# A decoder layer with a sparse expert FFN: x handed over turned, small inputs packed, the first projection unit in four pieces

## The chip, the cores and the metric

One core of a Trainium2 chip. The metric is the device time of one execution in microseconds (us). Engines: PE (TensorE, matmul; PEld its weight loads), DVE (VectorE), ACT (ScalarE), POOL (GpSimd), SP (SyncE, which only issues transfers here); SPq and ACTq are the issues of transfers from SP's and ACT's instruction streams. Each of the two has a queue of its own, and all transfers run on the core's 16 DMA engines.

## The reference

```python
h = rms_norm(x, attn_norm_g)                     # x: 256 tokens x 1024, float32
z = h @ w_in                                     # 1024 x 3640, one combined projection
(c_q, c_kv, k_pe, q_b, k_b, v_b, q_idx, k_idx, w_idx, gate_a, gate_b) = split_cols(z, IN_SPLITS)
y_a = mla_branch(...)                            # latent attention, 8 heads, causal
y_b = dsa_branch(...)                            # indexer scores -> 64 keys a query -> attention
merged = sigmoid(gate_a) * (y_a @ w_branch_mla) + sigmoid(gate_b) * (y_b @ w_branch_dsa)
x = x + merged @ w_out
x = x + moe_ffn(rms_norm(x, ffn_norm_g), ...)    # top 4 of 32 experts, 1024 -> 2x1024 -> 1024, with biases
return rms_norm(x, final_norm_g)
```

All is float32. The experts' weights are 32 x 12.6 MB, some 400 MB in all; the rest of the weights is about 25 MB.

## The kernel before, in words

The kernel is written engine by engine, with semaphores by hand; each engine runs its own list in the order written, so an engine waits where its list says.

*Front.* Tokens are two tiles t of 128 (`xs`). The model dimension is split into 8 slices c of 128; x and `w_in` are cut so that partition p holds elements 8p+c. The kernel needs h turned (`hT`, model dimension on the partitions). The scale 1/rms of a token is left out of h and is applied when a product leaves its PSUM bank; only the gain is multiplied in. So `turn_x(t)` (L631) turns tile t of x by 8 PE transposes with the identity into two banks, and DVE's `hidden(t)` (L1442) multiplies the two banks by `g_in` into `hT`. The combined projection is done in units of up to 512 columns: unit 0 is q_idx (512), unit 1 k_b, v_b, k_idx and w_idx (200 columns), unit 2 q_b (512), unit 3 c_q, c_kv and k_pe (416). `z_unit(n)` (L647) does, for each tile, 8 products of 128x128 by 128 x width into a bank of `ZB`; float32 makes each of them two passes in the trace. Unit 0's weights are loaded in three pieces (`Z_FIRST`, L74), and tile 1 of x is turned between slices 5 and 6 of tile 0. ACT's `z_evac(n)` (L1193) copies the banks out, scaled by the token's 1/rms; the bank of tile t of unit n has to be free (`z_ok`) before unit n+1 uses it. The scale comes from ACT (`Square` of x with a sum, L1180; root, L1189) and DVE (`x_rstd`, L1448). Between tile 0 and tile 1 of this, DVE works out the rotary angles from the positions and a second block of constants (L1460 to L1479), and ACT's list has both tiles' scales ahead of its first eviction. Two short products spread the scales over a row (`spread_rstd`, L638). PE runs ten passes on zeros at the start and four more behind the first turn (`open_clock`, L622).

*Small inputs.* ACT's queue brings the identity and `g_in` at once, the positions (two loads of one column) and the second constants behind the square of tile 0. SP's queue brings, in this order (L451, L487 to L502): x tile 0, the three pieces of unit 0, x tile 1, the constants ones and slot, unit 1 (two loads, strided rows), the gate-up biases in four loads, `g_q`, `g_kv`, the router's bias, units 2 and 3, `g_tok`, `b_down` four times, the up-projection weights (two loads), then gate, branch and output weights as slots of a ring of six come free. The gate-up biases (32 experts x 2048) are turned by four PE transposes between units 1 and 2 (L727 to L730) and put in their place (`bias_gu`) by two DVE copies (L1495). The router's weights and, column by column, `g_ffn` are loaded in the middle of the expert weights (L514 to L516) and multiplied together by DVE at L1623.

*Rest of the front.* Index scores, a top-64 search on DVE, up-projections, both attentions with gate products filled in between, branch products (L855), the output projection (L879), the residual, the router's logits (L894), the routing, and the gather of the first expert's tokens.

*Experts.* Each expert item takes up to 64 tokens: 4 units of gate-up weights and 2 of down weights, 2 MB each, through twelve slots that lie over the front's tiles. SP issues a load when PE has read the slot's last contents (`used`); before that, at L503 to L529, single loads are issued as parts of the front are finished with, the last one behind the logits (`lg_ps`, L528). Then `load_round` (L531) goes on with half and quarter loads behind the first products of the first expert (L556 to L562).

## Time and profile before

| | |
|---|---|
| runs, us | 1112.34, 1111.98, 1112.65; median 1112.34 |
| span of the profiled execution, us | 1110.8 |
| around the span, against the median, us | 1.5 |
| PE busy | 1075.1 us, 97% |
| DVE / ACT / POOL busy | 279.6 / 166.4 / 21.6 us |
| transferred | 431.67 MB, mean 389 GB/s |

The page gives the span of the profiled execution alone, not its own time with what lies around it. In the views, an engine's line reads: start, length, engine, line of the kernel, operation, written tile <- read tiles, number of instructions, and in brackets the idle time of the engine before it with what ended it. PE's ends are modelled, so "busy" can hold short waits. "issue" is time in which an engine waited for nothing that the profile shows.

### The profile page before, as it was taken

The numbers are of one execution on the slowest core, as the hardware profiler recorded it, in microseconds if no ns is written. First come the engines' busy times: TensorE is split into PE (matmuls) and PEld (weight loads), VectorE is DVE, ScalarE is ACT, GpSimd is POOL, SyncE is SP. The second block draws the span as 40 slices with busy tenths as digits, with TensorE's granted clock in tenths as the row PEclk, the third lists the DMA queues.
The fourth block names the chain that finished last, engine by engine and source line by source line (L and its number), as shares of the span: only waits on it lengthen the run. The fifth ranks groups of instructions, "written<-read, shape, count | busy, mean of one in ns | idle before, by whom it ended". The sixth has DMA issues, their size and how long they took to land.

```text
span 1110.8 us, 13188 instructions
## 1 busy us (share of the span) xinstructions
PE 1075.1 (97%) x5066; PEld 463.1 (42%) x5066; DVE 279.6 (25%) x658; ACT 166.4 (15%) x352; POOL 21.6 (2%) x44
## 2 busy tenths in 40 slices
PE   9999999999999999999999999999999999999997
PEld 6578786533333333333333333333333333333333
DVE  2167432322222222222222222222221111222112
ACT  2144430210110001101100100000000000000002
POOL 0121100000000000000000000000000000000000
PEclk9999999999999999999999999999999999999999
DMA  9934645899999999999999999999999999999997
GB/s 314 357 105 159 258 167 223 323 409 432 431 432 431 430 432 432 429 434 432 429 432 432 430 431 432 430 431 432 432 429 434 432 430 432 432 430 431 432 426 295
DMA packets 48085, 431.67 MB, mean 389 GB/s; under 512 B 8256, under 2 KB 10688, under 8 KB 23232
## 3 DMA queue, kind: packets, MB, share of 16 engines
q1 hardware_dynamic: 47200, 430.91, 92.4%
q10 hardware_dynamic: 864, 0.47, 0.1%
q8 instruction: 14, 0.23, 0.1%
q14 instruction: 7, 0.06, 0.0%
HBM read 430.32 MB, written 1.05 MB: 388 GB/s over the span
## 4 chain that ended last, share of the span: by engine, by line
PE 67%; DMA 22%; SPq 9%; DVE 1%; issue 0%; POOL 0%; ACT 0%; another core or an unknown queue 0%; POOLq 0%; DVEq 0%
PE bank L1033 26%; DMA raw<-in_w_gate_up 22%; PE bank L1056 12%; PE bank L615 8%; SPq L482 7%; PE bank L619 5%; PE bank L668 4%; PE bank L1005 3%; PE bank L955 3%; PE bank L883 2%; SPq L485 2%; PE bank L1072 1%; PE bank L689 1%; PE bank L677 0%; DMA cst<-in_consts 0%
## 5 line engine op out<-in xcount | busy, mean ns | idle before, releaser
L1033 PE MATMUL bank<-raw,xT 128*64 128x512 f32 x2048 | 461.9, 596 | 26.1 <-DMA raw<-in_w_gate_up 25.5
L1033 PEld LDWEIGHTS bank<-raw,xT 128*64 128x64 f32 x2048 | 141.5, 137 | 318.5 <-issue 264.9
L1056 PE MATMUL bank<-raw,actT 128*64 128x512 f32 x992 | 225.2, 595 | 0.0
L1056 PEld LDWEIGHTS bank<-raw,actT 128*64 128x64 f32 x992 | 68.7, 137 | 127.6 <-issue 119.0
L1693 DVE TENSOR_SCALAR gated<-cst,posc,gates 128x128 f32<-128x128 f32 x64 | 19.3, 344 | 278.2 <-PE bank L1005 278.2
L1744 DVE TENSOR_TENSOR gub<-bank,bias_gu 128x512 f32<-128x512 f32 x64 | 43.9, 685 | 160.4 <-PE bank L619 160.4
L1751 DVE COPY ev_gu<-bank 128x512 f32<-128x512 f32 x32 | 22.1, 692 | 219.4 <-PE bank L1033 219.4
L1352 ACT COPY ev_gu<-bank 128x512 f32<-128x512 f32 x32 | 18.7, 585 | 373.9 <-PE bank L1033 373.9
L1005 PE MATMUL bank<-ev,gated 64*128 64x512 f32 x248 | 61.6, 615 | 0.0
L615 PE MATMUL bank<-hT,front_raw 128*128 128x256 f32 x256 | 58.7, 382 | 0.0
L955 PE MATMUL bank<-x_res,onehot 128*64 128x512 f32 x248 | 58.5, 592 | 0.0
L615 PEld LDWEIGHTS bank<-hT,front_raw 128*128 128x128 f32 x256 | 47.4, 190 | 8.1 <-issue 2.3
L668 PE MATMUL bank<-front_raw,hT 128*128 128x512 f32 (+2 forms) x128 | 45.7, 516 | 0.0
L619 PEld LDWEIGHTS bank<-cst,ev_gu 128*128 128x128 f32 x256 | 33.4, 210 | 25.2 <-issue 25.2
L1357 ACT ACTIVATE ev_gu<-gub 128x512 f32<-128x512 f32 x32 | 20.1, 630 | 151.9 <-DVE gub L1758 151.9
L619 PE MATMUL bank<-cst,ev_gu 128*128 128x128 f32 x256 | 39.3, 297 | 0.0
L1005 PEld LDWEIGHTS bank<-ev,gated 64*128 64x128 f32 x248 | 21.3, 186 | 39.3 <-issue 39.3
L955 PEld LDWEIGHTS bank<-x_res,onehot 128*64 128x64 f32 x248 | 17.9, 137 | 35.3 <-issue 35.3
L668 PEld LDWEIGHTS bank<-front_raw,hT 128*128 128x128 f32 x128 | 23.9, 195 | 19.7 <-issue 19.4
L1362 ACT COPY ev<-bank 128x512 f32<-128x512 f32 x31 | 18.2, 586 | 81.6 <-PE bank L1056 81.6
L1331 ACT COPY ev<-bank 128x512 f32<-128x512 f32 x31 | 18.1, 585 | 73.3 <-PE bank L955 73.3
L1345 ACT COPY gated<-bank 128x256 f32<-128x256 f32 x32 | 11.9, 372 | 113.0 <-PE bank L619 113.0
(248 smaller groups left out, 598.9 us busy)
## 6 DMA issues: line engine op xcount, KB each, us to landing
raw<-in_w_gate_up SPq DMA_DIRECT2D x123, 2048.0 KB, 44.0
raw<-in_w_down SPq DMA_DIRECT2D x60, 2048.0 KB, 43.8
front_raw<-in_w_in SPq DMA_DIRECT2D x5, 2048.0 KB, 15.8
raw<-in_w_gate_up SPq DMA_DIRECT2D x9, 1024.0 KB, 9.2
raw<-in_w_down SPq DMA_DIRECT2D x12, 512.0 KB, 17.9
front_raw<-in_w_out SPq DMA_DIRECT2D x2, 2048.0 KB, 9.7
front_raw<-in_w_branch_mla SPq DMA_DIRECT2D x1, 2048.0 KB, 8.8
front_raw<-in_w_branch_dsa SPq DMA_DIRECT2D x1, 2048.0 KB, 7.8
```

Of the source, the lines that this page charges most:

```text
L482: sp.dma_start(raw[:, slot, :], w_gu_v[e, u // 2, :, u % 2 * UNIT:(u % 2 + 1) * UNIT]).then_inc(raw_in[slot], 16)
L485: sp.dma_start(raw[:, slot, :], w_dn_v[e, u]).then_inc(raw_in[slot], 16)
L615: mm = pe.matmul(o, lhs(c), rhs(c), start=start and c == 0, stop=c == n - 1)
L619: return pe.transpose(o, src, ident)
L668: mm = pe.matmul(ZB[t][:, 0:w], hT[:, c, t * P:(t + 1) * P], unit3(n, w)[:, c, :], start=c == 0, stop=c == KC - 1)
L883: mm = pe.matmul(B[2 * t + n][:, :], mT[:, c, t * P:(t + 1) * P], unit3(U_WO + n)[:, c, :], start=c == 0, stop=c == KC - 1)
L955: mm = pe.matmul(PREP[half * SLOTS:(half + 1) * SLOTS, :], onehot[:, t, :], xs[:, t, half * BLK:(half + 1) * BLK], start=t == 0, stop=t == ...
L1005: mm = pe.matmul(ACC[2 * t + half][:, :], scat[rows, t * P:(t + 1) * P], ev[rows, :], start=False, stop=True, skip_group_check=True)
L1033: mm = pe.matmul(GU[pair][half * SLOTS:(half + 1) * SLOTS, :], xT[:, c, b, :], w[:, at:at + BLK], start=u == 0 and k == 0, stop=last and k ...
L1056: mm = pe.matmul(DN[half * SLOTS:(half + 1) * SLOTS, :], actT[:, c, u, :], w[:, at:at + BLK], start=u == 0 and c == 0, stop=u == DN_UNITS ...
L1744: dve.tensor_tensor(gub[:, pair, :].rearrange("p (j s) -> p j s", s=SLOTS), GU[pair][:, :].rearrange("p (j s) -> p j s", s=SLOTS), bias_gu ...
L1751: dve.tensor_copy(ev_gu[:, 1, :], GU[1][:, :]).then_inc(lin_ev, 1)
```

## The change

The host hands the kernel other arrays (`laid_out`): x a second time, turned to partition p, slice c, token; `w_in` unit by unit, so that a unit is one contiguous row a partition; both up-projection weights in one array; the positions as one 128x2 array; the gate-up biases in the order of `bias_gu`; and `g_q`, `g_kv`, `g_ffn`, the router's bias and its weights in one array `packed`. On the chip, `hT` is loaded from the turned x in four pieces from ACT's queue and multiplied by `g_in` in place, slice by slice, for both tiles at once. PE's transposes of x and of the biases, the second `open_clock`, and the DVE copies of the biases go. Unit 0 comes in four pieces, in the order of the slices, each used for both tiles. Tile 0 of x is issued behind the third piece.

```diff
-Z_FIRST = (slice(0, 2), slice(2, 4), slice(4, KC))
+Z_FIRST = (slice(0, 1), slice(1, 2), slice(2, 4), slice(4, KC))
+IN_UNITS = Z_UNITS + [[(GATES_AT + k * BLK, BLK)] for k in range(4)]
+PACK = {"g_q": 2, "g_kv": 1, "g_ffn": KC, "rb": EXPERTS, "rw": KC * EXPERTS}
+def laid_out(inputs):
+    w = a["w_in"][0].reshape(P, KC, D_IN)
+    units = [np.concatenate([w[:, :, c0:c0 + n] for c0, n in part], axis=2).reshape(P, -1) for part in IN_UNITS]
...
+        "x_turned": a["x"][0].reshape(TOKENS, P, KC).transpose(1, 2, 0).reshape(P, KC * TOKENS),
+        "positions": a["positions"][0].reshape(TT, P).T,
+        "w_in": np.concatenate(units, axis=1),
+        "w_up": np.concatenate([a["mla_w_uq"][0].reshape(P, UP_Q), a["mla_w_ukv"][0]], axis=1),
+        "b_gate_up": a["b_gate_up"][0].reshape(EXPERTS, 2, 2, P, 4).transpose(3, 0, 1, 4, 2).reshape(P, EXPERTS * 16),
...
         def _(sp):
-            sp.dma_start(xs[:, 0, :], x[0, 0:P, :]).then_inc(x_in[0], 16)
...
-            load_front(0)
+            for cs, landed in zip(Z_FIRST, (*z_part, raw_in[0])):
+                sp.dma_start(unit3(0)[:, cs, :], w_in_v(0)[:, cs, :]).then_inc(landed, 16)
+                if cs.stop == KC // 2:
+                    sp.dma_start(xs[:, 0, :], x[0, 0:P, :]).then_inc(x_in[0], 16)
             sp.dma_start(xs[:, 1, :], x[0, P:2 * P, :]).then_inc(x_in[1], 16)
-            sp.dma_start(cst[:, P:KEPT], consts[:, P:KEPT]).then_inc(rest_in, 16)
             load_front(1)
-            for q in range(4):
-                sp.dma_start(bgu[q * EXPERTS:(q + 1) * EXPERTS, :], b_gate_up[0, :, q * BLK:(q + 1) * BLK]).then_inc(small_in, 16)
-            sp.dma_start(g_q[:, :], ...)
-            sp.dma_start(g_kv[:, :], ...)
-            sp.dma_start(rb[:, :], ...)
+            sp.dma_start(pack[:, :], packed).then_inc(small_in, 16)
             load_front(2)
             load_front(3)
             sp.dma_start(g_tok[:, :, :], ffn_norm_g[0].rearrange("(h p c) -> p h c", h=2, c=4)).then_inc(bd_in, 16)
+            sp.dma_start(bias_gu[:, :, :].rearrange("p e j -> p (e j)"), b_gate_up).then_inc(bias_in, 16)
...
-            sp.dma_start(rw[:, :, :], router_w[0].rearrange("(c p) n -> p c n", p=P)).then_inc(router_in, 16)
-            for c in range(KC):
-                sp.dma_start(g_ffn[:, c:c + 1], ...).then_inc(router_in, 16)
...
+            def first_z():
+                for cs, landed in zip(Z_FIRST[:-1], z_part):
+                    pe.wait_ge(landed, 16)
+                    for c in range(cs.start, cs.stop):
+                        pe.wait_ge(hT_ok, c + 1)
+                        for t in range(TT):
+                            z_product(0, t, c)
+                landed_front(pe, 0)
+                for t in range(TT):
+                    for c in range(Z_FIRST[-1].start, KC):
+                        if t == 0:
+                            pe.wait_ge(hT_ok, c + 1)
+                        mm = z_product(0, t, c)
+                    mm.then_inc(z_ps, 1)
...
-                    if t == 0 and n == 0:
-                        turn_x(0)
-                        open_clock(2)
...
-                        if n == 0 and t == 0 and c == 6:
-                            turn_x(1)
...
-            pe.wait_ge(small_in, SMALL)
-            for c in range(4):
-                tr = turned(B[7][:, c * P:(c + 1) * P], bgu[:, c:BLK:4])
-            tr.then_inc(bgu_ps, 1)
...
         def _(act):
-            act.dma_start(cst[:, 0:P], consts[:, 0:P]).then_inc(cst_in, 16)
-            act.dma_start(g_in[:, :], attn_norm_g[0].rearrange("(p c) -> p c", c=KC)).then_inc(g_in_in, 16)
+            act.dma_start(hT[:, Z_FIRST[0], :], xt_v[:, Z_FIRST[0], :]).then_inc(xt_in[0], 16)
+            act.dma_start(g_in[:, :], attn_norm_g).then_inc(g_in_in, 16)
+            for cs, landed in zip(Z_FIRST[1:], xt_in[1:]):
+                act.dma_start(hT[:, cs, :], xt_v[:, cs, :]).then_inc(landed, 16)
+            act.dma_start(cst[:, :], consts[:, 0:KEPT]).then_inc(cst_in, 16)
...
                 if t == 0:
-                    for k in range(TT):
-                        act.dma_start(pos_i[:, k:k + 1], positions[0, k * P:(k + 1) * P].rearrange("(p a) -> p a", a=1))\
-                            .then_inc(early_in, 16)
+                    act.dma_start(pos_i[:, :], positions).then_inc(early_in, 16)
                     act.dma_start(cst2[:, 0:sum(CONST.values()) - KEPT], consts[:, KEPT:]).then_inc(cst2_in, 16)
...
         def _(dve):
-            def hidden(t):
-                for k in range(2):
-                    dve.wait_ge(hT_ps, 2 * t + k + 1)
-                    dve.tensor_tensor(hT[:, 4 * k:4 * k + 4, t * P:(t + 1) * P], B[2 + 2 * t + k]..., ALU.mult).then_inc(hT_ok, 1)
+            def hidden(c):
+                dve.tensor_scalar(hT[:, c, :], hT[:, c, :], g_in[:, c:c + 1], None, ALU.mult).then_inc(hT_ok, 1)
...
+            for cs, landed in zip(Z_FIRST, xt_in):
+                dve.wait_ge(landed, 16)
+                for c in range(cs.start, cs.stop):
+                    hidden(c)
             dve.wait_ge(cst_in, 16)
-            hidden(0)
             x_rstd(0)
-            hidden(1)
-            dve.wait_ge(early_in, 32)
+            dve.wait_ge(early_in, 16)
             dve.wait_ge(cst2_in, 16)
...
-            dve.wait_ge(bgu_ps, 1)
-            for pair in range(2):
-                dve.tensor_copy(bias_gu[:, :, 8 * pair:8 * pair + 8]..., B[7]...).then_inc(bgu_ok, 1)
```

## Rows read from the trace of the kernel before

**Rows 1.** The page: busy time by engine, and the chain that ended last

```profile
PE 1075.1 (97%) x5066; PEld 463.1 (42%) x5066; DVE 279.6 (25%) x658; ACT 166.4 (15%) x352; POOL 21.6 (2%) x44
...
PE 67%; DMA 22%; SPq 9%; DVE 1%; issue 0%; POOL 0%; ACT 0%; another core or an unknown queue 0%; POOLq 0%; DVEq 0%
```

**Rows 2.** Stretches: length, busy time of each engine, PEclk, DMA share, GB/s

```profile
90.00:120.00 30.00, 30.00 (x191) 24.69 (x189) 20.69 (x55) 14.24 (x45) 4.34 (x6) 1.00 0.43 163
...
160.00:170.00 10.00, 10.00 (x48) 8.81 (x47) 3.33 (x6) 0.00 (x0) 0.00 (x0) 1.00 0.01 0
...
240.00:280.00 40.00, 40.00 (x192) 15.03 (x190) 8.87 (x19) 3.93 (x7) 0.00 (x0) 1.00 1.01 429
...
920.00:1020.00 100.00, 93.30 (x430) 32.44 (x432) 18.79 (x41) 8.68 (x17) 0.00 (x0) 1.00 1.01 432
```

**Rows 3.** Waits of the whole span: us in total, times, longest

```profile
PE bank L1033 <- DMA raw<-in_w_gate_up: 25.5, 39, 0.8
```

**Rows 4.** Issues of SP between 178 and 220 us, in order of time

```profile
178.47 1.28 SPq L482 DMA_DIRECT2D raw<-in_w_gate_up  x3
...
209.04 3.21 SPq L482 DMA_DIRECT2D raw<-in_w_gate_up  x2
219.36 0.33 SPq L556 DMA_DIRECT2D raw<-in_w_gate_up  x1
```

**Rows 5.** Waits of PE, 60 to 240 us: the longest of three

```profile
PE bank L1033 <- issue: 0.5, 1, 0.5
```

**Rows 6.** Chain that ended last within 0 to 60 us: start, us, what

```profile
4.62 1.97 PE bank L619 x8
...
7.45 6.08 PE bank L668 x12
13.53 0.89 PE bank L619 x8
14.41 14.00 PE bank L668 x52
...
28.86 0.48 PE bank L619 x4
29.33 13.73 PE bank L668 x32
```

**Rows 7.** Stretch 6 to 8 us, columns as in rows 2

```profile
6.00:8.00 2.00, 2.00 (x8) 1.57 (x7) 1.64 (x5) 0.20 (x1) 0.00 (x0) 1.00 1.05 381
```

**Rows 8.** The first microseconds in order of time

```profile
1.06 2.50 PE L625 MATMUL bank<-work 128*128 128x128 f32 x10 [1.06 <-DVE work L1438]
1.20 0.46 ACTq L1175 DMA_DIRECT2D g_in<-in_attn_norm_g  x1
...
5.67 0.83 ACTq L1185 DMA_DIRECT2D pos_i<-in_positions  x2
...
15.21 0.16 DVE L1462 CAST pos_f<-pos_i 128x2 f32<-128x2 int32 x1
...
18.24 0.67 ACT L1199 ACTIVATE area_k<-bank,stat 128x512 f32<-128x512 f32 x1
```

**Rows 9.** DVE, 0 to 30 us, groups by form: busy us, mean ns

```profile
L1454 DVE TENSOR_SCALAR area_k<-cst,stat 128x128 f32<-128x128 f32 x2 | 0.6, 286 | 0.1
```

**Rows 10.** Transfers by line: number, KB each, median us from issue to landing

```profile
front_raw<-in_w_in SPq DMA_DIRECT2D x5, 2048.0 KB, 15.8
...
cst<-in_consts ACTq DMA_DIRECT2D x1, 136.0 KB, 5.9
...
pos_i<-in_positions ACTq DMA_DIRECT2D x2, 0.5 KB, 5.7
g_in<-in_attn_norm_g ACTq DMA_DIRECT2D x1, 4.0 KB, 4.5
...
g_kv<-in_mla_kv_norm_g SPq DMA_DIRECT2D x1, 0.5 KB, 3.0
...
g_tok<-in_ffn_norm_g SPq DMA_DIRECT2D x1, 4.0 KB, 11.6
```

More of the change, by code:

```diff
@@ L82 @@
 GATES_FIRST = (6, 8, 10)
+IN_UNITS = Z_UNITS + [[(GATES_AT + k * BLK, BLK)] for k in range(4)]
+IN_WIDE = [sum(w for _, w in part) for part in IN_UNITS]
+IN_AT = [KC * sum(IN_WIDE[:k]) for k in range(len(IN_WIDE))]
+UP_Q = 2 * HEADS * QK
+UP_KV = HEADS * (NOPE + V_DIM)
+PACK = {"g_q": 2, "g_kv": 1, "g_ffn": KC, "rb": EXPERTS, "rw": KC * EXPERTS}
+PACK_AT = {}
+for _name, _n in PACK.items():
+    PACK_AT[_name] = sum(PACK[k] for k in PACK_AT)
 CONST = {"ident": P, "ones": P, "slot": P, "before": P, "causal": P, "invfreq": ROPE // 2}
@@ L185, in build @@
         g_in = fb("g_in", [P, KC])
[L186 to L188 removed]
+        pack = fb("pack", [P, sum(PACK.values())])
         pos_i = fb("pos_i", [P, TT], I32)
@@ L199, in build @@
         den = fb("den", [P, 2, 4])
-        rw = fb("rw", [P, KC, EXPERTS])
-        rb = fb("rb", [P, EXPERTS])
         front.close()
+        g_q, g_kv, g_ffn, rb = (pack[:, PACK_AT[k]:PACK_AT[k] + PACK[k]] for k in ("g_q", "g_kv", "g_ffn", "rb"))
+        rw = pack[:, PACK_AT["rw"]:PACK_AT["rw"] + PACK["rw"]].rearrange("p (c e) -> p c e", c=KC)
         raw = sb("raw", [P, SLOTS_W, UNIT])
@@ L238, in build @@
         small_in = sem("small_in")
-        SMALL = 16 * 7
-        router_in = sem("router_in")
+        bias_in = sem("bias_in")
+        xt_in = [sem(f"xt_in{k}") for k in range(len(Z_FIRST))]
         bd_in = sem("bd_in")
@@ L253, in build @@
         x_rs = sem("x_rs")
-        z_part = [sem(f"z_part{k}") for k in range(2)]
+        z_part = [sem(f"z_part{k}") for k in range(len(Z_FIRST) - 1)]
         warm_ok = sem("warm_ok")
@@ L383, in build @@
         br_w = [unit(U_BR + i)[:, 0:4 * D].rearrange("p (c n) -> p c n", c=4) for i in range(2)]
-        EXTRA = [16 if s in (1, U_UP % RING) else 0 for s in range(RING)]
         def landed_front(eng, n):
-            eng.wait_ge(raw_in[n % RING], 16 * (n // RING + 1) + EXTRA[n % RING])
+            eng.wait_ge(raw_in[n % RING], 16 * (n // RING + 1))
         def used_up(eng, n):
@@ L407, in arrived @@
         def arrived(slot):
-            return 16 * FRONT_LOADS[slot] + (EXTRA[slot] if slot < RING else 0)
+            return 16 * FRONT_LOADS[slot]
         def landed_expert(eng, j, place):
@@ L1899 @@
     arrays, args = {}, []
-    for name in _INS + ['consts']:
-        a = constants() if name == 'consts' else np.ascontiguousarray(inputs[name])
+    for name, a in laid_out(inputs).items():
+        a = np.ascontiguousarray(a)
         arrays[f"in_{name}"] = a
```

108 lines of the change are left out of this document (45 added, 63 removed).

## The prediction

> **What bounds the kernel now.** I read the page first, then stretches, waits, the issues of SP, and the chain and order of time of the first 45 us. The page has TensorE busy for 97% of the span and the chain that ended last as 67% PE and 22% DMA [rows 1]. An average over stages with different limits says little, so I cut the span [rows 2]. From 90 to 120 us PE is busy all the time and the DMA engines are loaded for less than a half. From 160 to 170 us nothing is loaded at all (0 GB/s), since every slot is full. From 240 us to 1020 us the rate stands at 429 to 432 GB/s whatever PE does: PE is fully busy at the start of that stretch and 93% busy at its end. The waits say why: PE waited 25.5 us, 39 times, for expert weights [rows 3]. So there are two regimes. The expert stage is one unbroken stream of weights at full rate, and its end is its start plus its bytes. Its start is set by PE: a load is issued at 209.04 us, behind the logits (L528), and the next at 219.36 us, behind the first expert products [rows 4]. That in turn is the end of a front stage in which PE has no gap worth the name: from 60 to 240 us there were three, the longest 0.5 us [rows 5]. A microsecond taken off PE's path in the front therefore moves the start of the stream, and the end, by a microsecond; one taken off a DMA, ACT or DVE in the front moves nothing, unless PE waits for it. The question is thus where PE stands when projection unit 1 and the bias turns are done.
>
> **The first 29 us of the kernel before.** PE's path there [rows 6]: it waits until 4.62 us for the identity, turns x tile 0, fills with four idle products, starts unit 0 at 7.45 us, turns x tile 1 in between (0.89 us), and has units 0 and 1 done at 14.41 + 14.00 = 28.41 us. A pass of a 512-wide float32 product costs 13.73 / 32 = 0.429 us (unit 2, at 29.33 us). Unit 0 is 32 such passes, 13.73 us, of which 12 run ahead of the turns and 20 behind them; unit 1 is the rest of the 52, 14.00 - 20 x 0.429 = 5.42 us. Together 19.15 us. The stretch from 7.45 to 28.41 us is 20.96 us; less 0.89 for the turns and 19.15 it leaves 0.92 us over. That is the slow clock: the first 12 passes took 6.08 us where 12 x 0.429 is 5.15, a loss of 0.93 us. The granted clock reads 1.00 in this stretch [rows 7], but the durations tell of half rate: ten 128-wide passes took 2.50 us at the start [rows 8], eight took 0.89 us at 13.53 us [rows 6]. I read that as 1.2 GHz and then 2.4 GHz. A loss of 0.93 us from 7.45 us on puts the rise at 7.45 + 2 x 0.93 = 9.3 us, 4.7 us after the run of work that began at 4.62 us and 8.2 us after the very first product at 1.06 us.
>
> **The change part by part.**
>
> x handed over turned: out go 16 transposes (8 ahead of unit 0, which count through its start; 8 inside it, 0.89 us), four idle products and the four DVE evictions behind them. In come eight DVE multiplications of 128x256 in place. The nearest row is 0.29 us for 128x128 from SBUF [rows 9]; twice that is the upper bound, I take 0.3 us, since the fixed part does not double. Only the first is on the path: the others have 1.7 us or more of product time each to hide behind.
>
> The new start. The first product needs piece 0 of x turned (128 KB), piece 0 of the weights (256 KB), the gains g_in and one multiplication. The two pieces are first in their queues. g_in is second behind x, as it was behind the identity: issued at 1.20 us [rows 8], it took 4.5 us, so it landed at 5.7 us. Small transfers took from 3.0 us on [rows 10], so the landing is between 4.2 and 5.7 us. It shared the engines with rows of 4 KB of x and has 2 KB rows of weights beside it now; I take 5.1 us, nearer to its own row. With 0.3 us of DVE and 0.2 us of hand-over PE starts at 5.6 us (4.7 to 6.2).
>
> The clock. PE does its ten idle passes until 3.56 us [rows 8] and nothing until 5.6 us. If the rise comes at 9.3 us as before, the loss is (9.3 - 5.6) / 2 = 1.85 us. If it comes 4.7 us after the start of the run, as before, it is 2.35 us. I take the middle, 2.1 us. The worst row is 8.2 us at half rate, a loss of 4.1 us. The Trainium skill, TensorE: Matmul & The Clock Gate, "What's actually happening", says that the throttled state is the default and activity releases it; that rule speaks against a change that leaves PE without work longer, and the trace agrees in so far as the rise came only behind the second run of work.
>
> Units 0 and 1 are then done at 5.6 + 19.15 + 2.1 = 26.85 us, not 28.41: 1.56 us saved. Each of the eight slices of unit 0 now serves both tiles before the next is needed, 4 x 0.429 = 1.7 us of work for 384 KB of weights and x, about 1.0 us at the 381 GB/s of this stretch [rows 7], so the pieces keep ahead.
>
> Gate-up biases laid out in the host: four 128-wide turns on PE go, 0.48 us at 28.86 us, right on the path between units 1 and 2 [rows 6]. The two DVE copies behind them and the load go beside PE's work; PE waits for neither, and they are worth nothing. The new load stands behind units 2 and 3 and is first read by the experts.
>
> Fewer and longer loads, and SP's queue: PE never waited for a load of the front, so neither is worth anything. The other way, there is 1 MB more to move, since x comes twice: up to the end of unit 1 these are 5.3 MB, 14 us at 381 GB/s and some 2 us of latency, so unit 1 lands near 16 us and PE reads it at 21.4 us. Covered. The router weights and the eight column loads of g_ffn leave SP's queue behind gate-up (1,0); the next load there waits for the branch products until 178.47 us anyway [rows 4]. Nothing. The constants ones and slot now come with the identity on ACT's queue behind x; DVE needs them for x's scale at some 13 us, where PE waits for nothing.
>
> Positions and second constants. ACT issues these behind the square of tile 0. That tile now stands behind 1 MB of weights, beside half of x turned: 2 MB, 5.5 us and 2 us of latency, so the issue moves from 5.67 us [rows 8] to some 9.5 and 10 us. With landing times as before, 5.7 and 5.9 us [rows 10], all are there at 15.9 us. DVE's angles begin then (at 15.21 us before), only behind them comes the scale of tile 1, and ACT's first eviction stands behind that; from 15.21 us to the end of this eviction at 18.91 us it was 3.7 us [rows 8]. So unit 0's first bank is free at 19.6 us, and PE asks for it at 5.6 + 13.73 + 2.1 = 21.4 us. Covered, by 1.8 us.
>
> **Sum.** 1.56 + 0.48 = 2.0 us. The bounds: start 4.7 us and rise at 9.3 us give 2.7 us; start 6.2 us and 8.2 us of half rate give -0.6 us. The span of the profiled execution is 1110.8 us, the median of the runs 1112.3 us; the 1.5 us around the span do not change. Forecast 1110.3 us. A measurement of this kernel tells about 0.2% from no change, 2.2 us, so the forecast lies just inside that bound.
>
> **Rivals.**
>
> (a) The start is dearer: the clock rises late, as in the worst row. For it: PE's gap grows from 1.05 us (3.56 to 4.61 us) to about 2 us. Against: one run of work was enough before, and z products are wider than the fillers. 1112.9 us; chance 0.07.
>
> (b) A new wait: PE at the first product of unit 1, for ACT's eviction of unit 0, for DVE's scale of tile 1, for positions and second constants. For it: on ACT's queue two 0.5 KB transfers needed 5.7 us where SP's 0.5 KB took 3.0 us [rows 10], and SP's queue now brings rows of up to 16 KB beside them; at 431 GB/s over 16 engines such a row takes 0.61 us, and if the queues take turns row by row, each of some 16 rows per engine on ACT's queue can wait that long. Against: unit 1 and the packed small inputs are due in that stretch, with rows of 6.4 and 1.2 KB. With the 11.6 us that the 4 KB g_tok took behind two large loads [rows 10], all are there at 21.6 us, the bank is free at 25.3, PE waits 3.9 us: 1114.2 us, chance 0.10. With the 15.8 us of a whole unit [rows 10]: 25.8 us, bank at 29.5, a wait of 8.1 us and 1118.4 us, slower than before; chance 0.05. The gain is gone from a landing at 19.7 us, and it is slower by 0.2% from 21.9 us. The Trainium skill, DMA: Bandwidth & Descriptors, "Queues, rings and completion order", says each engine goes round its queues packet by packet; by that rule this rival holds if the 16 KB rows are up by then, and no row here has such rows beside ACT's queue.
>
> (c) PE is earlier in the front, but the end does not move, since the stream of weights starts by something else. Against: its last two gates are PE's. 1112.3 us; chance 0.05.
>
> (d) The forecast, with a gain of 0.5 to 2.8 us: 0.73. It passes 2.2 us if the clock rises at 9.3 us (2.3 us then) or g_in lands before 5 us; that one of the two is so I hold for somewhat more likely than not: 0.43 of the 0.73, and 0.30 below.
>
> **Numbers.** The likeliest is 1110.3 us. 8 in 10: from 1109.1 us, a little better than the best bound, to 1112.4 us, which takes in (c) and the weak end of (d). Faster by over 0.2% 0.43, within 0.52 (0.30 + 0.07 + 0.10 + 0.05), slower 0.05.
>
> **What would show it.** First product of unit 0 at 5.6 us; passes of 0.85 us until 9 to 10.5 us, then 0.43; unit 0 done by 21.5 us; unit 2 at 27.3 us, 2.0 us earlier than 29.33; the issue behind the logits at 207.0 us; PE's waits for expert weights as before, and the end earlier by the same. A wait of PE for an eviction by ACT ahead of unit 1 shows (b); a later rise (a). I am wrong if unit 2 starts earlier and the issue behind the logits does not follow, or if the rate from 240 us on is another.

## The result, and the profile after

The changed kernel takes 1114.86 us (median of 12 runs, 1113.74 to 1117.8), the kernel before 1112.55 us (12 runs on the same chip, 1111.57 to 1113.86). The ratio is 1.0021, 95% interval 1.0014 to 1.0029: slower, by 2.3 us, where 1110.3 us was forecast. The time lies outside the range and close to what rival (b) gave for a landing at 21.6 us (1114.2 us).

The profiled execution took 1114.24 us with a span of 1112.2 us; the span before was 1110.8 us. Its page, in the lines that answer to [rows 1]:

```profile
PE 1072.8 (96%) x5042; PEld 459.7 (41%) x5042; DVE 279.1 (25%) x660; ACT 166.3 (15%) x352; POOL 21.7 (2%) x44
...
PE 62%; DMA 21%; SPq 15%; DVE 1%; issue 1%; ACT 0%; POOL 0%; ACTq 0%; DVEq 0%; POOLq 0%
```

PE is busy for 2.3 us less than before, as the transposes are gone, and the kernel is longer. The stretches that answer to [rows 2], columns as there:

```profile
240.00:280.00 40.00, 40.00 (x190) 15.12 (x188) 9.83 (x21) 3.93 (x7) 0.00 (x0) 1.00 1.01 429
...
920.00:1020.00 100.00, 92.76 (x430) 32.05 (x426) 19.36 (x42) 9.24 (x17) 0.00 (x0) 1.00 1.01 431
```

The second regime stands: one stream of weights at 429 to 431 GB/s, whatever PE does. The issues of SP behind the logits and behind the first expert products, beside [rows 4]:

```profile
209.99 3.21 SPq L510 DMA_DIRECT2D raw<-in_w_gate_up  x2
220.31 0.33 SPq L580 DMA_DIRECT2D raw<-in_w_gate_up  x1
```

They come 0.95 us later than before (209.04 and 219.36 us). So that much was lost ahead of 210 us. PE's waits of the whole span name the place ([rows 3] for before):

```profile
PE bank L1052 <- DMA raw<-in_w_gate_up: 26.1, 40, 0.9
PE bank L666 <- DVE hT L1464: 2.6, 1, 2.6
PE bank L666 <- ACT area_k L1219: 1.5, 1, 1.5
```

The waits for expert weights are what they were (26.1 and 25.5 us). The 2.6 us is the wait for unit 0's first multiplication, in the place of the waits around the turns. The third line is new: one wait of 1.5 us of PE, in the projections, for an eviction by ACT. The chain that ended last within 0 to 80 us tells what is behind it (start, us, what; [rows 6] before):

```profile
2.13 7.15 DMA x_res<-in_x
...
10.93 9.31 DMA cst<-in_consts
...
23.38 0.68 ACT area_k L1219
...
24.20 5.65 PE bank L666 x32
...
30.29 13.74 PE bank L666 x32
```

Read it upwards. Unit 2 begins at 30.29 us (29.33 before), behind unit 1 from 24.20 us, behind ACT's eviction, behind DVE's angles and scales (left out here), behind the second constants, which took 9.31 us from their issue at 10.93 us, behind ACT's square of x tile 0, behind the landing of that tile. No piece of TensorE stands between 2.13 and 24.20 us: the start of unit 1 is set by a transfer of 136 KB. The same in order of time, with what ended each idle time in brackets:

```profile
5.69 0.35 DVE L1464 TENSOR_SCALAR hT<-hT,g_in 128x256 f32<-128x256 f32 x1 [4.67 <-DMA g_in<-in_attn_norm_g]
6.19 16.55 PE L666 MATMUL bank<-front_raw,hT 128*128 128x512 f32 x32 [2.62 <-DVE hT L1464]
...
20.34 0.17 DVE L1482 CAST pos_f<-pos_i 128x2 f32<-128x2 int32 x1 [3.72 <-DMA cst<-in_consts]
...
24.20 5.65 PE L666 MATMUL bank<-front_raw,hT 128*128 128x200 f32 x32 [1.46 <-ACT area_k L1219]
```

PE has unit 0 done at 6.19 + 16.55 = 22.74 us and stands still for 1.46 us. DVE stood still for 3.72 us and began the angles at 20.34 us (15.21 before). The landings, beside [rows 10]:

```profile
cst<-in_consts ACTq DMA_DIRECT2D x1, 136.0 KB, 9.3
g_in<-in_attn_norm_g ACTq DMA_DIRECT2D x1, 4.0 KB, 4.5
```

The same 136 KB took 5.9 us before and 9.3 us now. They are 128 rows of 1088 bytes. In the kernel before, issued at 6.54 us, all of them were served between 11.0 and 11.9 us, beside rows of 512 and 1024 bytes of unit 1 and the constants on SP's queue, and the transfer landed at 12.5 us. In the changed kernel they are served from 15.9 us on, 5.0 us after the issue, when x turned, the first constants and the positions ahead of them are through. These are the stretches (columns as in rows 2), of the kernel before:

```profile
10.00:12.00 2.00, 2.00 (x6) 0.88 (x5) 0.00 (x0) 0.45 (x1) 0.00 (x0) 1.00 1.05 355
```

and of the changed kernel:

```profile
16.00:18.00 2.00, 2.00 (x6) 0.91 (x5) 0.45 (x2) 1.33 (x4) 0.00 (x0) 1.00 1.14 456
```

The DMA engines were fully loaded in both (shares 1.05 and 1.14), so the load alone is not the difference. What differs is what stands beside the constants. Up to 17 us they meet the packed inputs with rows of 1.2 KB, and 111 of the 128 rows are through. Then unit 2 comes up with rows of 16 KB, some 26 of which pass per microsecond: of the last 17 rows of the constants 13 are served in the microsecond from 17 us, 3 in the next, and the last at 19.24 us; the landing is at 20.24 us. Where both queues have work, an engine gives each a turn: in the microsecond from 10 us the trace has 34 rows of 8 KB from SP's queue and 33 rows of 4 KB from ACT's. The Trainium skill, DMA: Bandwidth & Descriptors, "Queues, rings and completion order", says that an engine goes round its queues packet by packet, a packet being some 9 to 17 descriptors. Of this the trace shows the turns, but mostly of one row each, and that is what is used here. It does not name the engine of a row, so this is read from rows that follow each other end to start.

It is tempting to blame the issues of SP, since units 2 and 3 are issued 9.7 us earlier than before. In the kernel before:

```profile
3.79 4.80 SPq L464 DMA_DIRECT2D front_raw<-in_w_in  x2
8.63 4.64 SPq L492 DMA_DIRECT2D x1T<-in_b_gate_up  x4
...
14.73 1.26 SPq L468 DMA_DIRECT2D front_raw<-in_w_in  x2
```

and the same two in the changed kernel:

```profile
5.01 1.06 SPq L498 DMA_DIRECT2D front_raw<-in_w_in  x2
```

But unit 2's first row is served at 16.05 us before and at 16.48 us now: more bytes stand ahead of it, and the earlier issue brings its rows no earlier. Unit 2 comes up at 16 us in either kernel. What the change did was to move the constants from 11 us into that stretch, and to make unit 2's rows 16 KB long in place of 2 KB.

### The profile page after: what moved, and what is told of

The parts are those of the page before. It is cut to its first block, busy times and chain, and to the rows that moved or that the text cites. A ratio compares the mean times of both kernels' runs of the same rounds, so it can differ in the third digit from the quotient of the medians.

```text
span 1112.2 us, 13118 instructions
## 1 busy us (share of the span) xinstructions
PE 1072.8 (96%) x5042; PEld 459.7 (41%) x5042; DVE 279.1 (25%) x660; ACT 166.3 (15%) x352; POOL 21.7 (2%) x44
## 3 DMA queue, kind: packets, MB, share of 16 engines
HBM read 431.36 MB, written 1.05 MB: 389 GB/s over the span
## 4 chain that ended last, share of the span: by engine, by line
PE 62%; DMA 21%; SPq 15%; DVE 1%; issue 1%; ACT 0%; POOL 0%; ACTq 0%; DVEq 0%; POOLq 0%
PE bank L1052 24%; DMA raw<-in_w_gate_up 18%; PE bank L1075 11%; PE bank L639 8%; SPq L510 7%; PE bank L643 5%; SPq L573 4%; SPq L513 3%; PE bank L974 3%; PE bank L1024 3%; PE bank L666 3%; PE bank L902 2%; DMA raw<-in_w_down 2%; DMA cst<-in_consts 1%; DMA x_res<-in_x 1%
## 5 line engine op out<-in xcount | busy, mean ns | idle before, releaser
L1052 PE MATMUL bank<-raw,xT 128*64 128x512 f32 x2048 | 461.9, 596 | 26.6 <-DMA raw<-in_w_gate_up 26.1
L1365 ACT COPY gated<-bank 128x256 f32<-128x256 f32 x32 | 11.9, 373 | 112.9 <-PE bank L643 112.9
```

The lines of the kernel that those rows point to most:

```text
L1052: mm = pe.matmul(GU[pair][half * SLOTS:(half + 1) * SLOTS, :], xT[:, c, b, :], w[:, at:at + BLK], start=u == 0 and k == 0, stop=last and k ...
```

## Two theories

**W, the wait.** The loss is PE's wait at unit 1 for ACT's eviction, through DVE's scale of tile 1, through the late second constants, whose lateness is due to the long rows on SP's queue. Take away either the dependence or the long rows and the kernel is faster than before by what the prediction's sum still leaves.

**C, the clock.** The loss is the slow clock: unit 0's 32 passes took 16.55 us, 2.8 us over 32 x 0.429 = 13.73, where the twelve ahead of the turns lost 0.93 us before [rows 6]. More idle products ahead of unit 0, until x is there, cure it.

In the expectations W is called T1 and C is called T2. A third, T3, is that the layout of the inputs in memory made the stream of the experts slower.

## Experiments

Four kernels ran on one chip beside the kernel before (1112.82 us, median of 33 runs). All the ratios below are to the kernel before on the same chip.

**The scale of tile 1 ahead of the angles.** Theory W's dependence is cut and nothing else: the constants may come as late as they like.

```diff
             x_rstd(0)
+            x_rstd(1)
             dve.wait_ge(early_in, 16)
...
-            x_rstd(1)
             dve.wait_ge(rstd_ps, 1)
```

> Edit to the changed kernel: DVE works out x's scale of tile 1 ahead of the rotary angles, not behind them, so ACT's first eviction no longer stands behind the positions and second constants. No transfer changes. Theory T1 (the change loses by PE's wait at unit 1 for that eviction, which hangs on the late constants): unit 1 starts as soon as unit 0 is done, 22.7 us in place of 24.2 in the profile, the wait of 1.5 us is gone, and the median falls from about 2.3 us over the kernel before to 0 to 0.8 us over it, since in the other runs the constants land later still. Rival T2 (the clock's late rise is the loss, 11.2 us against 9.3): unit 0 is done at the same time, and freeing the bank earlier gives the 1.5 us of the profile at most; if the spread of the runs is the clock's, it stays as wide as 1113.7 to 1117.8. Rival T3 (the stream of the experts is what got slower, by the layout of the inputs in memory): no gain in the end although unit 1 starts earlier.

1112.11 us (1111.72 to 1112.52, 11 runs), ratio 0.9995 [0.9986, 1.0004], span 1110.0 us. Its waits of PE, and its chain within 0 to 60 us:

```profile
PE bank L666 <- DVE hT L1464: 2.8, 1, 2.8
```

```profile
6.36 20.92 PE bank L666 x64
...
27.72 13.73 PE bank L666 x32
```

The wait for ACT is gone, units 0 and 1 are one unbroken run of 64 passes, and unit 2 begins at 27.72 us, 2.57 us earlier than in the changed kernel. Yet the constants come as late as there; this line of its order of time shows that they are no longer in anyone's way:

```profile
20.40 0.17 DVE L1483 CAST pos_f<-pos_i 128x2 f32<-128x2 int32 x1 [2.04 <-DMA cst<-in_consts]
```

The ratio falls from 1.0021 to 0.9995 and the intervals do not touch: 0.0026 x 1112.7 = 2.9 us. That is a little more than expected (0 to 0.8 us over the kernel before), and T3 falls: with the same layout in memory the end comes earlier. The run-to-run spread falls too, from 4.1 us between the lowest and the highest to 0.8 us.

**Twelve more idle products ahead of x.** Theory C's cure alone.

```diff
             pe.wait_ge(warm_ok, 1)
-            open_clock(5)
+            open_clock(11)
```

> Edit to the changed kernel: 11 idle products at the start in place of 5, so PE works until about 6 us, when the first slice of x is ready. T1: unit 0 is done earlier by half of the time by which the clock rises earlier (rise at 8 to 9.5 us: done 0.9 to 1.6 us earlier), but PE then waits that much longer for ACT's eviction of unit 0, whose time is set by the constants on ACT's queue: unit 1 starts at 24.2 us as in the changed kernel, and the end does not move (within 0.4 us). T2: the end comes 0.9 to 1.6 us earlier.

1115.47 us (1113.87 to 1116.16, 11 runs), ratio 1.0023 [1.0013, 1.0032], span 1112.6 us. PE in order of time:

```profile
6.24 3.98 PE L666 MATMUL bank<-front_raw,hT 128*128 128x512 f32 x8
11.36 10.54 PE L666 MATMUL bank<-front_raw,hT 128*128 128x512 f32 x24 [1.14 <-DVE hT L1464]
24.64 5.65 PE L666 MATMUL bank<-front_raw,hT 128*128 128x200 f32 x32 [2.74 <-ACT area_k L1219]
```

Unit 0 is done at 11.36 + 10.54 = 21.90 us, 0.84 us earlier than in the changed kernel, and PE then waits 2.74 us in place of 1.46. Theory C as the cause of the loss falls: with the wait in place, an earlier PE is worth nothing. It shows a third thing, too: PE now waits 1.14 us inside unit 0 for slices 2 and 3 of x.

**Both.** The scale first and 22 idle products.

> Both edits, scale first and 11 idle products. T1: the two losses add once the wait is gone: unit 1 starts at 21.2 to 21.9 us, 0.9 to 1.6 us ahead of scale first alone, and the median is 0.3 to 1.6 us below the kernel before. T2: as much below the changed kernel as the 11 idle products alone, plus 1.5 us. T3: at or over the kernel before.

1111.46 us (1110.89 to 1112.59, 11 runs), ratio 0.9985 [0.9976, 0.9994], span 1108.9 us. PE in order of time:

```profile
6.32 4.03 PE L666 MATMUL bank<-front_raw,hT 128*128 128x512 f32 x8 [0.89 <-DVE hT L1464]
11.19 15.95 PE L666 MATMUL bank<-front_raw,hT 128*128 128x512 f32 x56 [0.84 <-DVE hT L1464]
```

The clock is at its upper level for all of unit 0 (24 passes and unit 1 in 15.95 us are 24 x 0.429 + 5.65), and it helps little, as PE outruns its input: its passes stop at 10.35 us until slices 2 and 3 of x, on ACT's queue, have landed and been multiplied. Unit 2 begins at 27.58 us, 0.14 us earlier than without the added idle products. The two medians differ by 0.65 us, within the two intervals.

**Short rows on SP's queue.** Theory W's other half. Here the weights of units 2 and 3 are padded in memory by 16 columns per slice, so that each slice is a row of its own, of 2 KB or 1.6 KB. Same bytes, same order, and the scale of tile 1 again behind the angles.

```diff
-IN_AT = [KC * sum(IN_WIDE[:k]) for k in range(len(IN_WIDE))]
+IN_PAD = [16 if k in (2, 3) else 0 for k in range(len(IN_WIDE))]
+IN_ROW = [a + b for a, b in zip(IN_WIDE, IN_PAD)]
+IN_AT = [KC * sum(IN_ROW[:k]) for k in range(len(IN_WIDE))]
...
-            return w_in[:, IN_AT[k]:IN_AT[k] + KC * IN_WIDE[k]].rearrange("p (c n) -> p c n", c=KC)
+            return w_in[:, IN_AT[k]:IN_AT[k] + KC * IN_ROW[k]].rearrange("p (c n) -> p c n", c=KC)[:, :, 0:IN_WIDE[k]]
```

> Edit to the changed kernel: units 2 and 3 of w_in stand in memory with a gap of 16 columns behind each slice, so they are moved in rows of 2 KB (unit 2) and 1.6 KB (unit 3), as in the kernel before, in place of one row of 16 KB or 13 KB a partition. Everything else is the changed kernel, the DVE order too. If the constants are late because ACT's queue takes turns row by row with SP's 16 KB rows (the mechanism of rival b of the prediction), they land 1.5 to 3 us earlier than the 20.24 us of the changed kernel, PE's wait at unit 1 goes to 0 or nearly, the spread of the runs narrows, and the end is 1.5 to 2.3 us earlier. If they are late because their issue is late or ACT's queue is long in itself, they land within 0.7 us of 20.24 us and the end stays within 0.5 us.

1112.22 us (1111.37 to 1113.94, 11 runs), ratio 0.9993 [0.9984, 1.0002], span 1110.5 us. A landing, a line in order of time, and the chain:

```profile
cst<-in_consts ACTq DMA_DIRECT2D x1, 136.0 KB, 6.8
```

```profile
17.91 0.17 DVE L1485 CAST pos_f<-pos_i 128x2 f32<-128x2 int32 x1 [1.15 <-DMA cst<-in_consts]
...
20.95 0.67 ACT L1222 ACTIVATE area_k<-bank,stat 128x512 f32<-128x512 f32 x1
```

```profile
6.11 22.03 PE bank L669 x64
28.14 0.45 PE bank L661 x4
28.59 13.73 PE bank L669 x32
```

The same 136 KB land in 6.8 us and not 9.3; ACT's first eviction begins at 20.95 us, and PE, which asks for the bank at about 22.5 us, doesn't wait. The ratio is 3.1 us below that of the changed kernel (1.5 to 2.3 us expected). Two edits that share nothing, one of an order on DVE and one of the length of rows in memory, bring back the same 3 us. Theory W is shown in both its halves. The edit has a side effect: with the shorter rows SP's issue of unit 3 took 9.12 us, and all loads behind it were issued later. It does not touch the reading, since what stands beside the constants is unit 2, issued at 4.88 us (5.01 in the changed kernel) and served from 16.56 us (16.48). The spread of the runs narrows, as expected, but only from 4.1 to 2.6 us. The clock rose late in this profile (22.03 us where 64 passes at the upper level are 13.73 + 5.65 = 19.38), later than in the kernel with the scale first, 20.92 us; hence unit 2 at 28.59 against 27.72 us.

**What is left: the order of x.** The second set ran on another chip (before 1112.71 us, 31 runs). Since the piece with slices 2 and 3 of x, 256 KB on ACT's queue, paces unit 0 once the clock is up, this kernel, on top of both edits, puts pieces 1 to 3 of x on SP's queue, each ahead of the same slices' weights, and x itself behind unit 0. ACT's queue is then free for positions and second constants, which are issued at once. So three things change together: the queue of x turned, the place of 512 KB of x tile 0, and the place of the constants. No run separates them.

```diff
-            for cs, landed in zip(Z_FIRST, (*z_part, raw_in[0])):
+            for k, (cs, landed) in enumerate(zip(Z_FIRST, (*z_part, raw_in[0]))):
+                if k:
+                    sp.dma_start(hT[:, cs, :], xt_v[:, cs, :]).then_inc(xt_in[k], 16)
                 sp.dma_start(unit3(0)[:, cs, :], w_in_v(0)[:, cs, :]).then_inc(landed, 16)
-                if cs.stop == KC // 2:
-                    sp.dma_start(xs[:, 0, :], x[0, 0:P, :]).then_inc(x_in[0], 16)
+            sp.dma_start(xs[:, 0, :], x[0, 0:P, :]).then_inc(x_in[0], 16)
...
             act.dma_start(g_in[:, :], attn_norm_g).then_inc(g_in_in, 16)
-            for cs, landed in zip(Z_FIRST[1:], xt_in[1:]):
-                act.dma_start(hT[:, cs, :], xt_v[:, cs, :]).then_inc(landed, 16)
+            act.dma_start(pos_i[:, :], positions).then_inc(early_in, 16)
+            act.dma_start(cst2[:, 0:sum(CONST.values()) - KEPT], consts[:, KEPT:]).then_inc(cst2_in, 16)
```

> Edit on top of both (scale first, 11 idle products): pieces 1 to 3 of turned x go to SP's queue, each just ahead of the weights of the same slices, with both tiles of untouched x behind unit 0; the positions and second constants go on ACT's queue at once, behind g_in. In the trace of both edits PE waited for slices 2 and 3 of x, which landed at 10.7 us, after 1.5 MB that would need some 4 us. Theory T4 (rows on ACT's queue take turns with longer rows on SP's that nobody needs yet, and so x turned paces unit 0): slices 2 and 3 are there by 8 us, unit 0 runs without a gap and is done 1.0 to 1.5 us earlier, unit 2 starts at 26.1 to 26.6 us in place of 27.58, and the median falls to 1109.8 to 1110.6 us. Rival T5 (the order of the queues does not matter, the engines are simply full and x lands by bytes): slices 2 and 3 land within 0.7 us of before, no gain over both edits, median 1111.0 to 1111.8 us.

1110.14 us (1109.4 to 1111.55, 9 runs), ratio 0.9977 [0.9967, 0.9987], span 1108.6 us: the best of all, faster than both kernels. PE and DVE in order of time:

```profile
6.10 20.25 PE L667 MATMUL bank<-front_raw,hT 128*128 128x512 f32 x64
...
8.26 0.62 DVE L1462 TENSOR_SCALAR hT<-hT,g_in 128x256 f32<-128x256 f32 x2 [2.04 <-DMA hT<-in_x_turned]
```

Slices 2 and 3 are multiplied from 8.26 us and no longer from 10.7, and the second constants land in 6.3 us. Unit 2 begins at 26.79 us, a little later than the 26.1 to 26.6 us expected. The chain says what holds it now:

```profile
3.65 10.11 DMA front_raw<-in_w_in
...
13.80 12.55 PE bank L667 x48
```

PE is merged into one run from 6.10 us, but it holds two short waits for weights, the second until the last piece of unit 0, 1 MB, landed at 13.76 us. From there 48 passes follow without a stop. In this kernel it is the bytes ahead of the last slices that pace the front.

**The gains first.** The multiplication that starts unit 0 waits for g_in, so the edit exchanges the issues of g_in and of piece 0 of x.

> As x in order, with g_in ahead of the first piece of x on ACT's queue. In all changed kernels so far the first multiplication waited for g_in, which landed at 5.6 to 5.8 us, while the first x piece was there before. T4: g_in lands at 4.0 to 4.6 us, the first x piece now decides, at 4.6 to 5.4 us; the first product starts 0.4 to 1.0 us earlier than with x in order, and PE's 11 idle products may now be the gate (they end at about 5.4 to 6.1 us), so the end moves by 0 to 0.6 us. If g_in is slow for its 32-byte rows and not for its place, it lands after 5 us again and nothing moves.

1110.89 us (1110.29 to 1111.3, 11 runs), ratio 0.9983 [0.9974, 0.9992], span 1108.9 us. A miss. The landing of g_in, and the chain:

```profile
g_in<-in_attn_norm_g ACTq DMA_DIRECT2D x1, 4.0 KB, 3.0
```

```profile
3.56 10.71 DMA front_raw<-in_w_in
...
14.32 12.55 PE bank L667 x48
```

g_in lands in 3.0 us when it is first, and x now takes 4.7 us behind it: the pair is complete at 5.9 us and no longer at 5.6. But the chain does not go through the pair. The last piece of unit 0's weights landed at 14.27 us, 0.51 us later than with x in order (13.76), and unit 2 began at 27.31 us, 0.52 us later. Even a g_in that had come in time would have won nothing here. Why that piece landed later is not shown.

**The biases alone, in the kernel before.** The host lays the gate-up biases out; the four loads, four turns on PE and two copies on DVE are taken out, and nothing else is changed.

```diff
-            pe.wait_ge(small_in, SMALL)
-            for c in range(4):
-                tr = turned(B[7][:, c * P:(c + 1) * P], bgu[:, c:BLK:4])
-            tr.then_inc(bgu_ps, 1)
             z_unit(2)
```

> One part of the change alone, on the kernel before: the gate-up biases are laid out in the host and loaded into their place behind units 2 and 3; PE's four turns of them and DVE's two copies are gone, everything else is the kernel before. The prediction prices this at 0.48 us, on the path. All theories: unit 2 starts 0.45 to 0.6 us earlier than 29.33 us (give or take 0.5 us for the clock's rise), median 0.1 to 0.9 us below the kernel before in the same job.

1112.13 us (1111.6 to 1112.97, 11 runs), ratio 0.9994 [0.9985, 1.0003]: 0.6 us below before, and by its interval not told from nothing. The chain shows what the times can't:

```profile
7.26 6.53 PE bank L668 x12
...
28.67 0.44 PE bank L642 x4
29.11 13.74 PE bank L668 x32
```

Unit 2 follows directly on the four small products, and the 0.48 us of turns between them [rows 6] is gone. It begins only 0.22 us earlier than before, since the twelve passes at the start took 6.53 us here and 6.08 us there. SP's issues in this run show something else:

```profile
8.60 4.07 SPq L492 DMA_DIRECT2D g_q<-in_mla_q_norm_g  x1
```

In the kernel before, the four bias loads held SP for 4.64 us at this place. With them gone, the single small load that now stands there is held for 4.07 us, and units 2 and 3 are issued at 13.66 us, only 1.07 us earlier. The time was not the price of the bias loads: it reads as an issue that waits for what was issued before it, though the trace does not name the wait. Unit 1's two strided loads are the likely cause (their 2048 short rows are one row a partition in the changed kernel), but no run takes them out alone.

**Four more idle products in the kernel before.** open_clock(7) for open_clock(5), to ask what the clock alone is worth.

> The kernel before with 7 idle products at the start in place of 5, so that PE has no gap before the first turn of x at 4.6 us. If the clock's rise needs PE's work without a gap before it, it rises earlier than 9.3 us (at 4.5 to 8 us), the loss of 0.93 us in unit 0 goes partly or wholly, and the median is 0.3 to 1.0 us below the kernel before. If the rise is bound to the time and not to the gap, nothing moves (within 0.3 us).

1112.07 us (1110.97 to 1114.51, 11 runs), ratio 0.9995 [0.9986, 1.0005]. Inconclusive as a mean; the profile caught one end of it:

```profile
4.47 1.42 PE bank L619 x8
...
6.44 5.40 PE bank L668 x12
...
27.80 13.73 PE bank L668 x32
```

With the clock up before the turns were over (the turns start 0.21 us apart at first and 0.11 us apart from 5.2 us on), the twelve passes lose 5.40 - 5.15 = 0.25 us and not 0.93, and the turns take 1.42 us and not 1.97; unit 2 is at 27.80 us, 1.53 us earlier than before. That run took 1111.29 us; others of the same kernel took up to 1114.5 us. Whether more idle products raise the chance of an early rise is not shown by one trace; they do not fix its time.

**The constants issued early.** The last two ran on a third chip (before 1113.40 us, 21 runs). In the changed kernel, positions and second constants are issued at once behind the first ones, some 6 us earlier. If the issue time decides, the wait goes.

```diff
             act.dma_start(cst[:, :], consts[:, 0:KEPT]).then_inc(cst_in, 16)
+            act.dma_start(pos_i[:, :], positions).then_inc(early_in, 16)
+            act.dma_start(cst2[:, 0:sum(CONST.values()) - KEPT], consts[:, KEPT:]).then_inc(cst2_in, 16)
...
-                if t == 0:
-                    act.dma_start(pos_i[:, :], positions).then_inc(early_in, 16)
-                    act.dma_start(cst2[:, 0:sum(CONST.values()) - KEPT], consts[:, KEPT:]).then_inc(cst2_in, 16)
```

> Edit to the changed kernel: ACT issues the positions and second constants right behind its other constants, at some 4 us, in place of behind the square of tile 0 at 10.6 and 10.9 us. DVE's order is the changed kernel's. In ACT's queue they still stand behind x and the identity, which land at about 15.6 us, so the issue is 6 us earlier but the rows come only 1 to 3 us earlier. If the wait came from where these rows met SP's 16 KB rows (first ones served from 16 us on), they now go beside unit 1 and the packed inputs, land at 16 to 18.5 us, PE's wait at unit 1 is gone or under 0.3 us, and the median is 1.8 to 2.8 us below the changed kernel's 1114.9, as with scale first. If only x's scale behind the angles mattered and not the landing, 20 us stays and so does the time.

1114.28 us (1113.45 to 1116.25, 11 runs), ratio 1.0012 [1.0003, 1.0021], span 1112.7 us. A miss: the ratio is below the changed kernel's 1.0021, but the two intervals overlap, and PE waits 2.4 us in this profile. Its chain:

```profile
4.69 16.03 DMA cst<-in_consts
...
24.66 5.65 PE bank L666 x32
...
30.76 13.73 PE bank L666 x32
```

Issued at 4.69 us, the constants land at 20.72 us, 0.5 us later than when issued at 10.93. They queue on ACT's queue behind 1 MB of x turned and 192 KB of first constants. Their first row is served at 16.18 us, and the last ones still meet the 16 KB rows. So the later issue behind the square was not what mattered, as long as x turned stands ahead. In the kernel with x in order an early issue gives a landing in 6.3 us: of x turned only the first 128 KB are ahead of it.

**x in order, without the added idle products.** To part the two halves of the best version: its order with open_clock(5).

> x in order without the 6 added idle products (5 as in the kernel before), scale first kept. It splits the gain of x in order, 2.6 us below the kernel before, into the clock's term and the rest. If the slow clock is the price of an idle PE at the start, the rise comes at 9.5 to 12 us again, unit 0 loses 1.8 to 2.9 us to it in place of 0 to 0.6, but wins nothing from x being early in its first half; unit 2 starts 1.2 to 2.4 us later than 26.79 us and the median is 1111.3 to 1112.5 us, about that of scale first alone (1112.1), since at half rate PE did not wait for x there either. If the order of the queues is worth something by itself, it is over 0.5 us below scale first: under 1111.6.

1111.53 us (1110.65 to 1113.53, 11 runs), ratio 0.9985 [0.9976, 0.9994], span 1110.0 us. PE in order of time:

```profile
5.97 21.27 PE L667 MATMUL bank<-front_raw,hT 128*128 128x512 f32 x64 [2.40 <-DVE hT L1462]
```

Unit 2 begins at 27.68 us, the same as with the scale first alone (27.72 us). The 64 passes take 21.27 us against 20.25 with 22 idle products. In the profiles, idle products without the order gave 0.14 us (27.72 to 27.58), the order without them 0.04 us, both 0.93 us (27.72 to 26.79). That reads as if order and clock each needed the other, and the chains agree: here PE's passes decide from the first to the last, there the last weights did. But these are single profiles, and the clock's rise varies by more than these differences from one to the next. In the medians relative to before, the order without idle products stands at 0.9985, as low as idle products with the scale first; with three chips and intervals of 0.001 on each side, it is not settled.

## Why the prediction was wrong

**The step that failed** is the last of "Positions and second constants": "With landing times as before, 5.7 and 5.9 us [rows 10], all are there at 15.9 us ... Covered, by 1.8 us." They were there at 20.24 us. Of this, 0.9 us is the issue (10.93 for 10.0 us), 3.4 us the landing, 9.3 for 5.9. The transfer was moved into another stretch and its price kept. Of the 3.4 us, 0.5 is a longer wait behind its own queue (5.0 for 4.5 us), 2.4 the time from its first row to its last (3.3 for 0.9 us), and 0.4 the time from the last row to the landing. The stretch held unit 2, whose rows a part of the change had made eight times as long, and that part was costed at nothing: "Fewer and longer loads, and SP's queue". It asked whether PE waits for the long loads and found that it doesn't; it did not ask what their rows do to a transfer beside them. With unit 2's rows at 2 KB again the same constants landed at 17.82 us and PE did not wait. The prediction knew the mechanism, rival (b), with rows of 16 KB at 0.61 us each, and argued against it that unit 1 and the packed inputs, with shorter rows, are due "in that stretch". That was true of 111 of the 128 rows. But the last rows make a landing, and those met unit 2.

**Rival (b) was right in kind, its price in part by luck.** It took a landing at 21.6 us and PE's asking at 21.4 us, a wait of 3.9 us. The landing was 20.24 us and PE asked at 22.74 us, so the wait was 1.46 us. That the median came within 0.7 us of that rival's 1114.2 us is luck: the wait in the trace was shorter, and a later start, a later clock and runs slower than the traced one, which the rival did not have, made up for it. From the landing to unit 1 it is 24.20 - 20.24 = 3.96 us, 3.7 predicted.

**The account of unit 2,** 27.3 us predicted and 30.29 measured, 3.0 us apart:
- Start of unit 0: 6.19 us for 5.6, 0.6 us. The landing of g_in was taken as 5.1 us between 4.2 and 5.7, "nearer to its own row"; its own row, 4.5 us from issue, held to the digit. The multiplication and the hand-over were right (0.35 and 0.15 us for 0.3 and 0.2).
- Unit 0: 16.55 us for 13.73 + 2.1, 0.7 us. The clock rose later than both rows it was taken from; by the spacing of the passes, 0.85 us up to there and 0.43 us behind, at about 11.4 us. Rival (a)'s mechanism was there, at a third of its size (2.8 us lost, where the forecast had 2.1 and the rival 4.1).
- The wait: 1.46 us for nothing.
- Unit 1: 5.65 us for 5.42, 0.2 us. Its passes of 200 columns were priced by subtraction.

A further step held only by the slow clock: "so the pieces keep ahead". It compared rates and left out when the first bytes come. With the clock up, PE waited 1.14 us for slices 2 and 3 of x.

Without the wait the sum would have been 30.29 - 1.46 = 28.8 us, 0.5 us earlier than before and 1.5 us later than forecast. That is the weak end of case (d) even then, and the kernel with the short rows shows it: 28.59 us, ratio 0.9993.

**What held.** The bias turns: 0.48 us, shown by the biases alone. The multiplications of x, in place, beside the products. That a microsecond of PE in the front is one at the end: unit 2 0.96 us later, the issue behind the logits 0.95 us later. Over all the profiles: unit 2 at 26.79 us, a span of 1108.6 us; at 27.3 to 27.8, 1108.9 to 1110.0; at 28.59, 1110.5; at 29.1 and 29.3, 1111.2 and 1110.8; at 30.3 to 30.8, 1112.2 to 1112.7. The rate from 240 us on.

**Why slower by 2.3 us when the front lost 0.96 us.** The spans of the two profiles differ by 1.4 us; 0.96 is there at the logits. The rest comes at the start of the stream: the expert loads land 1.1 us later than before at 234 us and 1.4 to 1.5 us later from 244 us to the end, and PE shows it from about 650 us on, where it begins to wait for them. What costs these 0.5 us is not shown; it is of the size by which kernels with equal fronts differ (up to 1 us by the list above). The medians differ by 0.9 us more, since the profiled execution (1114.24 us) is among the faster of the twelve. The wait depends on two things that vary, the last rows' landing and the clock. In the two other profiles that have it, it was longer: 2.4 us with the constants issued early, 2.7 us with more idle products. That the untraced runs of the changed kernel had longer waits too is argued from this. The spread does not settle it: with the wait the lowest and highest runs lay 4.1, 2.8 and 2.3 us apart, without it 0.8, 1.7 and 2.6 us.

**Open.** When the clock rises. The granted clock reads 1.00 throughout and only durations tell. With ten idle products and a start of unit 0 between 5.97 and 6.4 us, the passes went from the lower rate to the upper at about 11.4 us in the changed kernel and with short rows, at 10.3 us with the constants issued early, at 9.7 us with x in order, and at 9.4 us with the scale first. With 22 idle products it was about 4.5 us in one kernel (they took 4.37 us), 5.3 us in another (4.75 us), and between 6.2 and 6.9 us in two more (5.06 and 5.07 us). No run here separates kernel from chance in this.

## What to carry to other kernels

A small transfer's time to land is not its own: it belongs to the rows beside it on the other queue and to what is ahead on its own. So when a change moves it, or makes the rows of another stream longer, price it anew in the stretch in which its last row will stand. Small work that gates an eviction goes ahead of work that waits for late data, even where that data has always been early. And what TensorE consumes in pairs, a slice of x and its weights, was best put on one queue in the order of use: that, with x itself behind the weights and TensorE kept at work until the first pair was there, gave 1110.14 us, 0.9977 of the kernel before.

## What the runs showed that was not expected

- Two queues take turns on the DMA engines by rows and not by bytes: 136 KB in rows of about 1 KB landed in 9.3 us when their last rows met rows of 16 KB, and in 6.8 us when they met the same bytes in rows of 2 KB.
- Issuing 6 us earlier did not land anything earlier (20.72 against 20.24 us) when a megabyte stood ahead on the same queue, and issuing units 2 and 3 9.7 us earlier did not bring up unit 2's rows any earlier (16.48 against 16.05 us).
- A long issue is not the price of what is issued: SP was held for 4.64 us at the bias loads, and for 4.07 us at a 1 KB load once they were gone.
- TensorE kept busy with 22 idle products from 1.06 us on had its upper rate at about 4.5 us in one run and only after 6.2 us in others; the kernel before, with pauses, at 9.3 us.
